# Three-instruction correction of the inverse root, and one transfer for the samples' y

## What is computed

```python
def _rmsnorm(x, g):
    y = xf * lax.rsqrt(jnp.mean(xf * xf, axis=-1, keepdims=True) + EPS) * g
...
h = _rmsnorm(x, norm_mix); proj = h @ w_in        # attention and S5 branches follow
x = x + merged @ w_out
x = x + _conv_ffn(_rmsnorm(x, norm_ffn), ...)     # w_up, causal conv, SiLU gate, w_down
...
y_prompt = _rmsnorm(xp, norm_final)               # (1, 256, 2048)
y_sample = _rmsnorm(xs, norm_final)               # (8, 4, 2048)
```

## Time and profile before

| what | us |
|---|---|
| runs (three) | 1545.87, 1548.26, 1551.14; median 1548.26 |
| profiled execution | 1549.25 |
| its span in the trace | 1547.4 |
| PE busy | 1532.3 (99%) |
| DVE busy | 1027.2 (66%) |
| ACT busy | 660.6 (43%) |
| POOL busy | 463.3 (30%) |

### The profile page before, as it was taken

The page is one execution under the profiler, slowest core; times in us unless marked ns, Lnnn a source line. Parts: engine busy times, 40 slices in busy tenths (PEclk is TensorE's granted clock), DMA queues, the critical chain, the costliest instruction groups (busy, mean ns, idle before and its releaser), DMA issues.

```text
span 1547.4 us, 33798 instructions
## 1 busy us (share of the span) xinstructions
PE 1532.3 (99%) x12498; PEld 1515.2 (98%) x12498; DVE 1027.2 (66%) x1475; ACT 660.6 (43%) x866; POOL 463.3 (30%) x581
## 2 busy tenths in 40 slices
PE   8999999999999999999999999999999999999998
PEld 8999999999899999999999999999999999999998
DVE  7756788888576666667776767677777764444443
ACT  6334345545566634444333434333333333333332
POOL 8993368877332201221111111111111100001100
PEclk9999999999999999999999999999999999999999
DMA  8887476666766586556555555554545465555552
GB/s 264 243 181 207 140 217 201 199 206 188 225 205 202 166 198 226 163 180 207 164 163 163 163 163 163 162 169 157 176 149 180 147 222 180 176 174 172 171 172 89
DMA packets 298990, 282.16 MB, mean 182 GB/s; under 512 B 35072, under 2 KB 290576, under 8 KB 298768
## 3 DMA queue, kind: packets, MB, share of 16 engines
q1 hardware_dynamic: 283008, 256.69, 54.9%
q10 hardware_dynamic: 13568, 16.62, 3.4%
q0 software_dynamic: 2320, 7.54, 1.5%
HBM read 266.73 MB, written 14.05 MB: 181 GB/s over the span
## 4 chain that ended last, share of the span: by engine, by line
PE 90%; POOL 5%; SPq 1%; DVE 1%; DMA 1%; issue 1%; ACT 0%; POOLq 0%; DVEq 0%; ACTq 0%
PE banks L571 29%; PE banks L573 29%; PE banks L572 29%; POOL angle L1830 1%; POOL angle L1833 1%; PE banks L581 1%; POOL sm L1830 1%; DVE wlo L1273 1%; POOL sm L1833 1%; PE banks L699 1%; DMA raw<-in_w_in 1%; PE banks L778 0%; PE banks L737 0%; POOL rdec L1830 0%; DMA raw<-in_w_glu 0%
## 5 line engine op out<-in xcount | busy, mean ns | idle before, releaser
L1273 DVE TENSOR_TENSOR wlo<-raw,whi 128x1024 fp32r<-128x1024 f32 x443 | 559.8, 1278 | 287.0 <-ACT whi L916 282.6
L916 ACT ACTIVATE whi<-raw 128x1024 fp32r<-128x1024 f32 x443 | 461.8, 1051 | 545.2 <-PE banks L573 492.9
L572 PE MATMUL banks<-h_lo,whi 128*128 128x288 f32 x1408 | 415.7, 295 | 0.0
L573 PE MATMUL banks<-h_hi,wlo 128*128 128x288 f32 x1408 | 415.7, 295 | 0.0
L571 PE MATMUL banks<-h_hi,whi 128*128 128x288 f32 x1408 | 414.6, 294 | 0.0
L571 PE MATMUL banks<-hhi,whi 128*128 128x288 f32 (+1 forms) x912 | 271.3, 297 | 4.3 <-DVE hlo L1299 3.3
L573 PE MATMUL banks<-hhi,wlo 128*128 128x288 f32 (+1 forms) x912 | 269.1, 295 | 0.0
L572 PE MATMUL banks<-hlo,whi 128*128 128x288 f32 (+1 forms) x912 | 269.0, 295 | 0.0
L572 PEld LDWEIGHTS banks<-h_lo,whi 128*128 128x128 f32 x1408 | 264.6, 188 | 0.1
L573 PEld LDWEIGHTS banks<-h_hi,wlo 128*128 128x128 f32 x1408 | 264.4, 188 | 0.0
L571 PEld LDWEIGHTS banks<-h_hi,whi 128*128 128x128 f32 x1408 | 264.1, 188 | 0.1
(11 more groups left out here) (339 smaller groups left out, 2166.4 us busy)
## 6 DMA issues: line engine op xcount, KB each, us to landing
raw<-in_w_up SPq DMA_DIRECT2D x352, 256.0 KB, 3.4
raw<-in_w_in SPq DMA_DIRECT2D x223, 256.0 KB, 3.4
raw<-in_w_down SPq DMA_DIRECT2D x176, 256.0 KB, 3.0
raw<-in_w_glu SPq DMA_DIRECT2D x64, 256.0 KB, 3.2
raw<-in_w_out SPq DMA_DIRECT2D x64, 256.0 KB, 3.3
raw<-in_w_attn_proj SPq DMA_DIRECT2D x32, 256.0 KB, 4.0
scratch_gates<-gt ACTq DMA_DIRECT2D x16, 288.0 KB, 3.6
gbt<-scratch_gates POOLq DMA_DIRECT2D x8, 288.0 KB, 3.4
```

The lines of the kernel that those rows point to most:

```text
L572: pe.matmul(out, h, xl[:, kt, :], start=False, stop=False)
L573: mm = pe.matmul(out, lo, xh[:, kt, :], start=False, stop=kt == nk - 1)
L916: act.activation(whi[:, s, :, 0:cols], raw[:, s, :, 0:cols], ACT.Copy).then_inc(hi_ready, 1)
L1273: dve.tensor_tensor(wlo[:, s, :, 0:cols], raw[:, s, :, 0:cols], whi[:, s, :, 0:cols], ALU.subtract).then_inc(lo_ready, 1)
```

## The change

The correction is written with a fused instruction: DVE computes t = (y * -0.5) * y, then t = t * v, and the caller computes (t + 1.5) * y, so that the separate multiply-and-add goes, in all three places. The four stores of the samples' y become one, from 128 partitions to a destination walked as 4 column blocks (j) of 32 rows of 512 columns, and the final wait counts one transfer.

```diff
             act.wait_ge(sem("yo_ready1"), 4)
-            for j in range(4):
-                act.dma_start(O["y_sample"][:, 4 * P * j:4 * P * (j + 1)], yo[TS * j:TS * (j + 1), 7, :]).then_inc(sem("ys_stored"), 16)
+            act.dma_start(O["y_sample"].rearrange("r (j c) -> j r c", j=4), yo[:, 7, :]).then_inc(sem("ys_stored"), 16)
             act.wait_ge(sem("y_stored"), 16 * 6)
-            act.wait_ge(sem("ys_stored"), 16 * 4)
+            act.wait_ge(sem("ys_stored"), 16)
...
                 meanwhile()
-                own.link(dve.tensor_tensor(t, y, y, ALU.mult))
+                own.link(dve.scalar_tensor_tensor(t, y, -0.5, y, ALU.mult, ALU.mult))
                 own.link(dve.tensor_tensor(t, t, v, ALU.mult))
-                own.link(dve.tensor_scalar(t, t, -0.5, 1.5, ALU.mult, ALU.add))
...
-            own.link(dve.tensor_tensor(rstd[:, :], nw[1][:, :], rstd[:, :], ALU.mult))
+            own.link(dve.scalar_tensor_tensor(rstd[:, :], rstd[:, :], 1.5, nw[1][:, :], ALU.add, ALU.mult))
...
-            dve.tensor_tensor(rtok[:, 4:7], rtok[:, 4:7], nw[0][:, 0:3], ALU.mult).then_inc(sem("rtok_ready"), 1)
+            dve.scalar_tensor_tensor(rtok[:, 4:7], nw[0][:, 0:3], 1.5, rtok[:, 4:7], ALU.add, ALU.mult).then_inc(sem("rtok_ready"), 1)
```

## The result

| kernel | median us | runs | ratio to the kernel before, 95% interval |
|---|---|---|---|
| before | 1547.51 | 12 | 1 |
| after | 1550.99 | 12 | 1.0021 [1.0014, 1.0028] |

The ratio stands for 3.2 us (2.2 to 4.3). The forecast was 1549.7 us, +1.4 us, with a range of 1546.4 to 1551.8: the sign and the range held, the size was less than half of what came. It is still a change within the 0.3% that I had called "the same".

A forecast was written before the change was run, and what follows sets the result against it. Bound: PE's matmul queue, then the tail's DMA drain. Extra 48 KB per engine less 0.8 us gave +1.2 to +1.6, taken as +1.4 us; on the 1548.26 us median, 1549.7 us, range 1546.4 to 1551.8.

The forecast's parts named there:

- The bound: Whole run: PE's matmul queue is full around the first two roots; the tail is bound by DMA engines draining 2.36 MB.
- The two roots of 288 columns at nothing: Roots near 37 and 702 us: each 0.24 us shorter on DVE, counted at nothing behind an ACT wait and full PE.
- the 0.05 us per fused instruction: 288-column roots on DVE: each fused instruction, at 512 ns, takes 0.05 us more than a plain one, twice per root.
- The third root: Tail, 3 columns: root ends 0.10 to 0.20 us earlier, so first store and drain start earlier, counted as -0.15 us.
- Four engines: Tail, merged y_sample store: runs on 4 DMA engines, 13508 packets on ACT's queue, DMA share near 0.25; chance 0.72.
- Rival 1: Tail: the merged store uses all 16 engines, priced at -0.7 us, 1547.6 us; chance 0.12.
- rival 2: Tail: four engines, but the extra data is hidden by faster engines, -0.4 to +0.4 us, 1548.3 us; chance 0.10.
- rival 3: Tail: store falls to fewer than 4 engines, slower beyond noise, +4.9 us at two, 1558 us at one; chance 0.03.
- The price of the extra 48 KB: Tail: each of four engines carries 48 KB more of y_sample, costing 2.0 to 2.4 us at 24.3 to 20.3 GB/s.
- The credit of 0.8 us: Tail: 0.8 us taken off the 48 KB cost for the earlier start and the lost stragglers of the late fourth issue.
- The signs: Trace: 80 to 100 GB/s in the tail with SP's queue empty; 13520 packets or a span under 1547.4 us would refute.
- the worse rate: Tail: 15.6 GB/s per engine, from the slowest half microsecond, makes the 48 KB cost 3.2 us, +2.4 us; kept for the range.

The follow-up runs named there:

- roots_only: Against the kernel before: only the three fused roots, with the four y_sample stores kept; 1547.67 us, ratio 1.0005.
- roots_again: Repeat of the kernel with only the three fused roots and the four old stores, against the kernel before; 1547.13 us, ratio 1.0000.
- flat_store: Against the kernel before: old roots, one y_sample store to 128 plain rows of 512 numbers, on 16 engines, output blocks in another order; 1547.58 us, ratio 1.0000.
- store_only: Against the kernel before: only the single y_sample store to four blocks, on 4 engines, with the old roots; 1549.46 us, ratio 1.0013.
- two_stores: Against the kernel before: old roots, y_sample in two stores of 64 partitions, each to two blocks, both on the same 2 engines; 1552.66 us, ratio 1.0038.
- gap_blocks: Against the kernel before: old roots, one four-block store on 4 engines, output laid out so a block's rows lie 2 KB apart; 1549.84 us, ratio 1.0014.
- store_alone: Against the kernel before: old roots, the four-block store on 4 engines issued only after all y_prompt stores have landed; 1552.18 us, ratio 1.0030.
- flat_again: Against the kernel before: old roots, one store to 128 plain rows on 16 engines, output put in order by the host; 1547.39 us, ratio 1.0001.

## Why the prediction was right, and where it was not

- **The bound.** PE is full from 36 to 44 and from 700 to 710 us after as before, and the tail answered to the change: 15.4 us from the first transpose on in place of 11.7. Right.
- **The two roots of 288 columns at nothing.** Right as far as roots_only and roots_again can tell: 1.0005 and 1.0000, each to about 1.3 us. Their own saving was larger than my 0.24 us, 0.36 at the first: the fused kind costs 460 ns, not the 512 that I took from a group with another type of output. The mis-sized term is the 0.05 us per fused instruction; it is 0.
- **The third root.** In the tail, on 3 columns, the first step before and the three steps after:

```profile
1536.64 0.16 DVE L1321 TENSOR_TENSOR newton<-rtok 128x3 f32<-128x3 f32 x1
...
1532.90 0.16 DVE L1320 SCALAR_TENSOR_TENSOR newton<-rtok 128x3 f32<-128x3 f32 x1
1533.10 0.16 DVE L1321 TENSOR_TENSOR newton<-newton,rtok 128x3 f32<-128x3 f32 x1
1533.29 0.16 DVE L1787 SCALAR_TENSOR_TENSOR rtok<-newton,rtok 128x3 f32<-128x3 f32 x1
1533.49 0.75 DVE L1792 TENSOR_SCALAR yo<-banks,rtok 128x512 f32<-128x512 f32 x1
```

  From its first step to the first scaled bank it is 0.59 us, where it was 0.80 (1536.64 to 1537.44): the full 0.20 us sooner, the upper end of my 0.10 to 0.20. A gain of that size in the whole time can't be told from noise.
- **Four engines.** Right: 13508 packets, a share near a quarter, and no landing figure. Rival 1 (all 16) is refuted by the packets and by flat_store, which shows what it would have given (1.0000, where I had priced it at -0.7 us); rival 2 (hidden, -0.4 to +0.4 us) by the result itself and by store_only (+0.8 us at least); rival 3 came true only where I built it, in two_stores.
- **The price of the extra 48 KB.** This is the first term that was too small. I took 2.0 to 2.4 us at 20.3 to 24.3 GB/s for one engine, from stretches in which mostly the prompt's packets moved. The samples' own packets are slower. Added up, the 128 of them took 15.6 us before, about 1.0 us for each of 16 engines, and 17.1 us after, about 4.3 us for each of four (16.9 in store_only, 16.3 in gap_blocks, 16.2 in store_alone). The difference, 3.1 to 3.3 us, is what the 48 KB cost, an estimate from these sums. For two_stores the same estimate is 13.7 / 2 - 1.0 = 5.9 us, and it measured +5.9. The right rate stood in my rows: 15.6 GB/s for one engine in the slowest half microsecond, 3.2 us for the 48 KB. Nine of the samples' 18 slow packets start in that half microsecond, and I kept it for the range because it was short.
- **The credit of 0.8 us.** This is the second mis-sized term, with the other sign. I took off 0.15 us for the earlier start and about 0.65 us for the late packets, which I put down to the late fourth issue. The four kernels with a single issue on 16 engines have the same tail as the three with four issues (11.4 to 11.7 us against 11.3 to 11.7) and the same time, and flat_store still has late packets of the prompt, the last of them ending at 1544.3, 0.8 us behind its full stretch. So late packets come without a late issue, and the credit is near nothing. With both terms as measured the sum is 3.2 - 0 = +3.2 us in place of +1.4. The whole change gave +3.2 and +3.1; the three four-engine kernels with old roots gave +2.0 to +2.3, with intervals that reach 3.4 to 3.7.
- **The signs.** I expected 80 to 100 GB/s in the tail, with SP's queue empty. It showed 71 and 75, and SP's last store landed only at 1545.5. I had also written that a span under 1547.4 us would be wrong, and the profile after has 1547.3. That was a bad sign to choose: the executions of the kernel before alone lie between 1545.87 and 1551.14 us, further apart than the whole effect is large.
- **The range** held the result (1550.99 against 1551.8) since it left room for the worse rate, +2.4 us, and for the scatter of the runs. The change was forecast 1.8 us too small. The time was off by 1.3 us only (1549.7 against 1550.99), because the three runs that I started from had a median 0.75 us above that of the twelve: that part is luck.

## What to carry to other kernels

Fewer transfers are not fewer microseconds: where the end of a kernel drains at a full DMA share, count the bytes of the busiest DMA engine. Before two transfers are merged, look at the first dimension of both sides: here 4 blocks against 128 partitions put 256 KB on 4 engines, while four transfers of 32 rows had used all 16. The trace tells it before anything is built, from the small completion packets of a transfer of the same shape, and from a missing landing figure. And where the rate of one engine is needed, take it from packets of the same transfer, not from the mean of a stretch in which others dominate.

## What the hardware showed that I had not expected

- The transfer on four engines started slowly even with nothing beside it (store_alone: 28 GB/s over two microseconds, then 91). Its slow packets are not its own: the four stores of 32 rows before have as many, and a plain store of 128 rows has none.
- The issue of 128 rows on ACT took 0.35 us when the destination was plain and 1.17 us in four blocks. The four issues of 32 rows before took 3.19 us together, so the blocks are not all that counts.
- PE's granted clock was 0.50 (1.2 GHz) from 1532.2 to 1535.5 in the execution after, behind a stretch in which PE had worked on the one-column sums (L864, L866) and on the first of the transposes. The 28 transposes of the prompt took 4.94 us there and 3.28 us at 1.00 (2.4 GHz) in the execution before: 1.7 us. Of the 14 profiles 7 have such a stretch near 12, 414 or 1533 us (flat_again has two) and 7 have none; in the execution before it came at 414, after PE had waited 2.3 us for DVE. In the tail it delayed PE's last transposes and not the end: flat_again, with the 4.94 us, has 11.5 us from the first transpose to the end of the span, where flat_store has 11.4 with 3.28. So an event behind such a stretch is a bad start for a comparison of two tails.
